# Latent-attention mixer on one core: the next head's queries and keys turned in four halves, in another PSUM bank

## The reference, cut to what matters

```python
def attend(qblk):                      # 128 queries at a time
    s = jnp.einsum('bqhd,bkhd->bhqk', qblk, k, preferred_element_type=jnp.float32) * scale
    p = jax.nn.softmax(s, axis=-1)
    return jnp.einsum('bhqk,bkhd->bqhd', p.astype(v.dtype), v)

o = lax.map(attend, qb)
...
y = jnp.einsum('bsm,md->bsd', jnp.concatenate([y_pool, y_attn], axis=-1), w_out[l])
```

## Time and profile before

| | us |
|---|---|
| median of 3 runs | 2757.69 |
| lowest, highest | 2755.79, 2765.08 |
| the profiled execution, its own time | 2761.88 |
| its span | 2760.1 |
| PE busy in the span | 2582.2 |
| DVE busy | 1772.6 |
| ACT busy | 1045.2 |
| POOL busy | 1052.5 |

### The profile page before, as it was taken

One profiled execution on the slowest core, in us unless ns is written; L12 is line 12 of the kernel. 1 busy time (PEld: TensorE's weight loads), 2 busy tenths in 40 slices (PEclk: granted clock), 3 DMA queues, 4 the chain that ended last, 5 costly groups with the idle time before them and its releaser, 6 DMA issues.

```text
span 2760.1 us, 40033 instructions
## 1 busy us (share of the span) xinstructions
PE 2582.2 (94%) x15932; PEld 2230.6 (81%) x15932; DVE 1772.6 (64%) x2506; ACT 1045.2 (38%) x1797; POOL 1052.5 (38%) x734
## 2 busy tenths in 40 slices
PE   6899999989999999999999999999999898688888
PEld 5788899966678899999998877777888786577777
DVE  6876776646433389795776346666333698777763
ACT  4322323321134332222223346666343335566651
POOL 1554554500044454554544520000344465344444
PEclk9999999999999999999999999999999999799999
DMA  6445444652024334433323374441342333000023
GB/s 237 126 173 179 139 157 141 229 205 93 24 100 154 105 109 155 142 127 107 116 91 109 115 226 123 118 131 46 122 152 100 120 114 114 1 1 1 31 77 145
DMA packets 241414, 328.09 MB, mean 119 GB/s; under 512 B 19134, under 2 KB 178110, under 8 KB 239436
## 3 DMA queue, kind: packets, MB, share of 16 engines
q1 hardware_dynamic: 239756, 325.42, 35.3%
q10 hardware_dynamic: 1472, 0.10, 0.0%
HBM read 246.16 MB, written 79.33 MB: 118 GB/s over the span
## 4 chain that ended last, share of the span: by engine, by line
PE 71%; DVE 15%; issue 6%; ACT 3%; DMA 3%; POOL 1%; SPq 0%; DVEq 0%; ACTq 0%
PE ps L851 18%; PE ps L853 18%; PE ps L852 18%; PE ps L996 4%; DVE raw L1675 3%; PE ps L984 2%; PE ps L1080 2%; DMA raw<-in_w 2%; PE ps L1060 2%; PE ps L1194 2%; PE ps L1068 1%; PE ps L1044 1%; DVE u L1689 1%; DVE st L2200 1%; PE ps L1207 1%
## 5 line engine op out<-in xcount | busy, mean ns | idle before, releaser
L807 POOL TENSOR_TENSOR w_lo<-raw,w_hi 128x512 fp32r<-128x512 f32 (+1 forms) x576 | 848.5, 1482 | 1438.1 <-ACT w_hi L1264 1437.5
L1264 ACT ACTIVATE w_hi<-raw 128x512 fp32r<-128x512 f32 (+1 forms) x580 | 357.4, 628 | 1052.1 <-PE ps L853 815.4
L851 PE MATMUL ps<-w_hi,s_hi 128*128 128x256 f32 (+1 forms) x1344 | 383.6, 285 | 10.5 <-POOL w_lo L807 10.5
L853 PE MATMUL ps<-w_hi,s_lo 128*128 128x256 f32 (+1 forms) x1344 | 381.9, 284 | 0.0
L852 PE MATMUL ps<-w_lo,s_hi 128*128 128x256 f32 (+1 forms) x1344 | 381.8, 284 | 0.0
L851 PE MATMUL ps<-w_hi,a_hi 128*128 128x256 f32 (+1 forms) x1008 | 286.2, 284 | 6.6 <-DVE a_lo L1645 4.4
L1689 DVE TENSOR_TENSOR u<-u,ps 128x1024 f32<-128x1024 f32 (+1 forms) x128 | 155.3, 1213 | 204.7 <-PE ps L853 200.8
L852 PE MATMUL ps<-w_lo,a_hi 128*128 128x256 f32 (+1 forms) x1008 | 285.9, 284 | 0.0
L853 PE MATMUL ps<-w_hi,a_lo 128*128 128x256 f32 (+1 forms) x1008 | 285.8, 284 | 0.0
L851 PEld LDWEIGHTS ps<-w_hi,s_hi 128*128 128x128 f32 x1344 | 260.1, 194 | 21.4 <-issue 19.5
L853 PEld LDWEIGHTS ps<-w_hi,s_lo 128*128 128x128 f32 x1344 | 260.1, 193 | 0.0
(11 more groups left out here) (280 smaller groups left out, 5687.1 us busy)
## 6 DMA issues: line engine op xcount, KB each, us to landing
raw<-in_w SPq DMA_DIRECT2D x191, 512.0 KB, 4.0
ada_c<-in_ada SPq DMA_DIRECT2D x14, 2304.0 KB, 10.7
blk<-u SPq DMA_DIRECT2D x62, 512.0 KB, 3.4
blk<-c SPq DMA_DIRECT2D x31, 512.0 KB, 3.3
blk<-m1s SPq DMA_DIRECT2D x31, 512.0 KB, 3.4
ada_first<-in_ada SPq DMA_DIRECT2D x12, 768.0 KB, 15.9
r_g<-blk SPq DMA_DIRECT2D x8, 1024.0 KB, 9.2
r_v<-blk SPq DMA_DIRECT2D x4, 2048.0 KB, 11.5
```

The source lines that it names most:

```text
L807: pool.tensor_tensor(w_ring(w_lo, n), w_source(n), w_ring(w_hi, n).bitcast(F32), ALU.subtract)\
L851: pe.matmul(out, a_hi_, b_hi_, start=first, stop=False, skip_group_check=True)
L853: return pe.matmul(out, a_lo_, b_hi_, start=False, stop=last, skip_group_check=True)
L1264: act.activation(w_ring(w_hi, n), w_source(n), ACT.Copy).then_inc(w_rounded, 1)
```

## The change

The queries and keys of the next head are turned in four halves of 512 tokens (queries low and high, keys low and high) at i = 2, 3, 4 and 5, each into bank 7 alone. Banks 4 and 5 hold turned probabilities alone. For the first head the four halves go to banks 4, 5, 6 and 7. Each half waits for the half before it to be read by DVE (`l_hlow`), from the third head on also for the gate of the values that bank 7 held (`l_gated`, 2h - 2). The values that go to bank 7 wait for the last half, and so do the first scores of the next head. New semaphores `l_hturned` and `l_hlow` count halves; `l_pevac` and `l_pdone` count probabilities alone.

The orders change too. PE issues scores of e + 2, then the half, then the turn of e, then the values. ACT copies the probabilities, takes the exponentials of e + 2 and then copies the half. DVE takes the maxima of e + 2, writes the probabilities' low part, inverts the sum of e + 2 and then writes the half's low part; at i = 5 (and at i = 1, where no half is turned) the gate follows.

Apart from this, the three semaphores of the DMAs of `ada_first[1]` become one, PE waits for the keys on `l_kchain` in place of `l_kdone`, and SP's wait ahead of the output weights becomes one for both halves of the last head's queries, that is at i = 3 of head 6.

```diff
-        ada_in = [[sem(f"ada_in{n}{c}") for c in range(3)] for n in range(4)]
+        ada_in = [[sem(f"ada_in{n}{c}") for c in range(3)] for n in (0, 2, 3)]
+        ada_second = sem("ada_second")
...
-        def l_head_bank(n):
-            bank = 6 if n == 1 else 4
-            return psf[0:LQK, bank * 512:bank * 512 + S].rearrange("p (m n) -> p m n", m=NT)
+        L_HALVES = {2: (0, 0), 3: (0, 1), 4: (1, 0), 5: (1, 1)}
+
+        def l_head_bank(h, k, c):
+            return ps[0:LQK, 7 if h else 4 + 2 * k + c].rearrange("p (m n) -> p m n", m=4)
+
+        def l_head_half(h, k, c, low):
+            return l_t[h % 2][k][low][0:LQK, 4 * c:4 * c + 4]
+
+        def l_half_count(h, k, c):
+            return 4 * h + 2 * k + c + 1
...
-                sp.wait_ge(l_pdone, 2 * head_unit(LH, LH - 1, 0) + 2)
+                sp.wait_ge(l_hturned, l_half_count(LH - 1, 0, 1))
...
-            for c in range(3):
-                pe.wait_ge(ada_in[1][c], 16)
+            pe.wait_ge(ada_second, 16 * 3)
...
-                pe.wait_ge(l_kdone, 1)
-
-                def l_turn_head(h, k):
-                    n = head_unit(LH, h, k)
-                    if n > 1:
-                        pe.wait_ge(l_pevac, 2 * n)
-                    for m in range(NT):
-                        tr = pe.transpose(l_head_bank(n)[:, m], (l_k if k else l_q)[:, m, h * LQK:(h + 1) * LQK],
-                                          ident[:, :])
-                    tr.then_inc(l_pdone, 2)
+                pe.wait_ge(l_kchain, 4 * NT)
+
+                def l_turn_head(h, k, c):
+                    if h:
+                        pe.wait_ge(l_hlow, l_half_count(h, k, c) - 1)
+                    if h > 1:
+                        pe.wait_ge(l_gated, 2 * h - 2)
+                    for m in range(4):
+                        tr = pe.transpose(l_head_bank(h, k, c)[:, m],
+                                          (l_k if k else l_q)[:, 4 * c + m, h * LQK:(h + 1) * LQK], ident[:, :])
+                    tr.then_inc(l_hturned, 1)
...
                     if i == 0:
-                        pe.wait_ge(l_pevac, 2 * head_unit(LH, h, 1) + 2)
+                        pe.wait_ge(l_hlow, 4 * h + 4)
...
-                    pe.wait_ge(l_pevac, 2 * prob_unit(LH, 2 * pair + 1) + 2)
+                    pe.wait_ge(l_pevac, 4 * pair + 4)
+                    if i == NT // 2 and h + 1 < LH:
+                        pe.wait_ge(l_hlow, 4 * h + 8)
...
                 for e in range(LH * NT):
                     h, i = divmod(e, NT)
-                    turned_head = h + 1 < LH and i - 1 in TURN_AT[LH]
                     if e + 2 < LH * NT:
                         l_scores(e + 2)
-                    if turned_head:
-                        l_turn_head(h + 1, TURN_AT[LH].index(i - 1))
+                    if h + 1 < LH and i in L_HALVES:
+                        l_turn_head(h + 1, *L_HALVES[i])
+                    l_turn(e)
+                    if e and e % 2 == 0:
                         l_values(e // 2 - 1)
-                        l_turn(e)
-                    else:
-                        l_turn(e)
-                        if e and e % 2 == 0:
-                            l_values(e // 2 - 1)
...
-                    if h + 1 < LH and i - 1 in TURN_AT[LH]:
-                        l_head_turned(h + 1, TURN_AT[LH].index(i - 1))
+                    l_prob_turned(e)
+                    if e + 2 < LH * NT:
                         l_exps(e + 2)
-                        l_prob_turned(e)
-                    else:
-                        l_prob_turned(e)
-                        if e + 2 < LH * NT:
-                            l_exps(e + 2)
+                    if h + 1 < LH and i in L_HALVES:
+                        l_head_turned(h + 1, *L_HALVES[i])
...
-                    if turned_head:
-                        l_head_low(h + 1, TURN_AT[LH].index(i - 1))
+                    l_prob_low(e)
+                    if e + 2 < LH * NT:
                         l_inverse(e + 2)
-                        l_prob_low(e)
-                    else:
-                        l_prob_low(e)
-                        if e + 2 < LH * NT:
-                            l_inverse(e + 2)
+                    if h + 1 < LH and i in L_HALVES:
+                        l_head_low(h + 1, *L_HALVES[i])
                     if h and i == 1:
                         l_gate(h - 1, 1)
                     if i == 5:
```

More of the change, by code:

```diff
@@ L295, in build_program @@
         (l_pads, l_sums, l_roots, l_latok, l_diff, l_ydone, l_yready, l_lturned, l_lhi, l_llo, l_rcopied,
-         l_updone, l_upfree, l_sq, l_rr, l_qdone, l_kdone, l_kchain, l_sdone, l_max, l_neg, l_exp, l_rinv, l_prob,
-         l_vhi, l_vfree, l_phi, l_half_ok, l_headhi, l_pdone, l_pevac, l_odone, l_gated) = (
+         l_updone, l_upfree, l_sq, l_rr, l_qdone, l_kchain, l_sdone, l_max, l_neg, l_exp, l_rinv, l_prob,
+         l_vhi, l_vfree, l_phi, l_half_ok, l_hturned, l_headhi, l_hlow, l_pdone, l_pevac, l_odone, l_gated) = (
             sem(n) for n in ("l_pads", "l_sums", "l_roots", "l_latok", "l_diff", "l_ydone", "l_yready",
                              "l_lturned", "l_lhi", "l_llo", "l_rcopied", "l_updone", "l_upfree", "l_sq", "l_rr",
-                             "l_qdone", "l_kdone", "l_kchain", "l_sdone", "l_max", "l_neg", "l_exp", "l_rinv",
-                             "l_prob", "l_vhi", "l_vfree", "l_phi", "l_half_ok", "l_headhi", "l_pdone", "l_pevac", "l_odone", "l_gated"))
+                             "l_qdone", "l_kchain", "l_sdone", "l_max", "l_neg", "l_exp", "l_rinv",
+                             "l_prob", "l_vhi", "l_vfree", "l_phi", "l_half_ok", "l_hturned", "l_headhi", "l_hlow", "l_pdone", "l_pevac", "l_odone", "l_gated"))
         def product_end(s, i):
@@ L632, in _ @@
                     sp.dma_start(ada_first[n][:, 3 * c:3 * c + 3], t["ada"][n][:, 3 * c:3 * c + 3])\
-                        .then_inc(ada_in[n][c], 16)
+                        .then_inc(ada_in[(0, None, 1, 2)[n]][c] if n != 1 else ada_second, 16)
             load_raw(R11, 0)
@@ L834, in _ @@
                         key_rope(m)
-                    pool.sem_inc(l_kdone, 1)
                     for e in range(LH * NT):
@@ L1191, in l_turn @@
                     for c in range(2):
-                        pe.wait_ge(l_pevac, 2 * prob_unit(LH, e) + c - 1)
+                        if e:
+                            pe.wait_ge(l_pevac, 2 * e + c - 1)
+                        else:
+                            pe.wait_ge(l_hlow, 4)
                         for n in range(4 * c, 4 * c + 4):
@@ L1210, in l_values @@
                     mm.then_inc(l_odone, 1)
-                l_turn_head(0, 0)
-                l_turn_head(0, 1)
+                for k in range(2):
+                    for c in range(2):
+                        l_turn_head(0, k, c)
                 l_scores(0)
@@ L1234, in l_between @@
                     if q == 1 and k == 0:
-                        pe.wait_ge(l_pevac, 2 * prob_unit(LH, LH * NT - 1) + 2)
+                        pe.wait_ge(l_pevac, 2 * LH * NT)
                         pe.wait_ge(l_gated, 2 * LH)
@@ L1559, in _, with l_head_turned @@
                 l_root(2 * NT - 1)
[L1561 to L1564, removed]
+                def l_head_turned(h, k, c):
+                    act.wait_ge(l_hturned, l_half_count(h, k, c))
+                    act.activation(l_head_half(h, k, c, 0), l_head_bank(h, k, c), ACT.Identity,
                                    scale=gains[0:LQK, 10 + k:11 + k]).then_inc(l_headhi, 1)
@@ L1570, in l_exps @@
                     if e >= 3:
-                        act.wait_ge(l_pdone, 2 * prob_unit(LH, e - 3) + 2)
+                        act.wait_ge(l_pdone, 2 * (e - 3) + 2)
                     act.activation(l_p[:, e % 3], psf[:, (e % 2) * 1024:(e % 2) * 1024 + S], ACT.Exp,
@@ L1578, in l_prob_turned @@
                     for c in range(2):
-                        act.wait_ge(l_pdone, 2 * prob_unit(LH, e) + c + 1)
+                        act.wait_ge(l_pdone, 2 * e + c + 1)
                         if e >= 4:
@@ L1590, in l_other_half @@
                     act.activation(l_half[l_rows(h), :], ps[l_rows(h + 1), 6 + a], ACT.Copy).then_inc(l_half_ok, 1)
-                l_head_turned(0, 0)
-                l_head_turned(0, 1)
+                for k in range(2):
+                    for c in range(2):
+                        l_head_turned(0, k, c)
                 l_exps(0)
@@ L1865, in _ @@
                     if k % 3 == 0:
-                        dve.wait_ge(ada_in[piece][k // 3], 16)
+                        dve.wait_ge(ada_in[n][k // 3], 16)
                     src = ada_first[piece][:, k]
@@ L2227, in l_gate, with l_head_low @@
                     dve.tensor_tensor(tile, high, tile, ALU.mult).then_inc(l_gated, 1)
[L2229 to L2236, removed]
+                def l_head_low(h, k, c):
+                    dve.wait_ge(l_headhi, l_half_count(h, k, c))
```

(6 more changed lines are left out.)

## The result

The changed kernel takes 2812.41 us (median of 4, 2810.34 to 2816.68) against 2756.74: 1.0201 times as long, 95% interval 1.0185 to 1.0218. The forecast had the sign, but its time was 2788.4 and its range ended at 2800: the loss is 55.7 us where 30.7 were forecast.

A forecast was written before the change was run, and what follows sets the result against it. The prediction took a chain of waits in the attention tiles to bound the kernel, no engine being full. 2761.88 + 18.2 (chain) + 12.5 (clock) = 2792.6 us profiled, less 4.2 for a median: 2788.4, range 2770 to 2800.

The forecast's parts named there:

- What bounds the kernel: Third mixer's 64 attention tiles: no engine full, a chain of waits counts; shared banks 4 and 5 make 27.9 us of them.
- The rounds: Halves at i = 2 to 5, each waiting for the one before in bank 7: 4.9 us each, 19.6 a head.
- The first scores of the next head: At i = 6 they wait for the last low part; from there to the next gate at i = 1, 18.2 us.
- The chain in sum: A head takes 37.8 us against 34.9 at full clock; seven heads, less 1.1 at each end, give +18.2 us.
- 20.4 and 12.5: Us added in attention: 20.4 for seven heads of 2.9 more, 12.5 for nine more clock falls of 1.4.
- The clock: TensorE falls to 1.2 GHz after two long pauses a head: 14 falls instead of 5, +12.5 us.
- My discount from 1.6 to 1.4: Us charged per clock fall in attention, lowered because in a round PE does only a part of the chain.
- The faster rival: Attention halves fit idle ACT and DVE time, rounds under 4.2 us overlap, 27.9 us gained: 2730 us; chance 0.05.
- The range: Whole kernel: 2770 us, without more falls and with rounds 0.2 shorter, up to 2800, nearly all falls; leaves out some 0.16.
- the case of falls after all three pauses: Attention clock also falls after the third pause, or halves are slower: 2801.5 us and up; chance 0.06.
- At no cost: Start's single DMA wait, `l_kchain` and SP's later output weight loads cost nothing; the loads at most 5.3 us if uncovered.

The follow-up runs named there:

- the two filled kernels: Throwaway transposes put into PE's pauses: the changed kernel with three pauses a head filled, 2768.6 us; the kernel before with its one pause filled, 2756.21 us.
- the best kernel: The changed kernel with the half first in ACT's and DVE's queues and bank 7 gated at i = 0: 2724.54 us, ratio 0.989.

## Why the prediction was right or wrong

*What bounds the kernel*: right. No engine was full, the chain of waits decided, and the 22.1 us of waits for the shared banks went away without a gain.

*The rounds*: right. 4.9 us against 4.79 measured at full clock. Inside, the half's copy and low part were taken too cheap, 0.60 and 0.66 against 0.68 and 0.75; the other pieces came out shorter by as much and more. The lesson of the miss is that a half of the longer copy's time, 0.55 and 0.64, is too low a guide: the time shrank less than the size.

*The first scores of the next head*: right. Pause 3.6 forecast, 3.27 measured. From rounds and head at full clock, 37.4 - 4 x 4.79 = 18.2 us remain for the rest of a head, just the 18.2 of the forecast.

*The chain in sum*: +18.2 forecast, +13.4 measured between the two filled kernels, some 11 without the fillers' own cost. The forecast counted seven heads of 2.9. Between the first and the last gate of bank 7 lie six, 2.4 longer each, +14.7; from there to the last gate the changed kernel, filled, is 2.8 shorter (24.5 against 27.3), where I took off 1.1. At the start turning to scores gave back 1.0 (2370.90 to 2376.08 is 5.2 us, before 6.2), forecast 1.1. The sum was too high, for the heads' sake. (The prediction's 20.4 and 12.5 are 20.3 and 12.6 by its own factors, which changes nothing.)

*The clock*: this step failed. Its sign and mechanism were right and its size was not. "I take a fall after each of the two long ones: 14 instead of 5, 9 x 1.4 = 12.5 us", on top of what before lost already, measured 41.8 - 6.4 = 35.4 us in the stage, some 37 without the fillers' cost. Two of its factors were too small. The count: 21 falls, three a head, the upper end that I had named, against 14. The length: by the clock of 0.81 a steady head has 2 x 0.19 x 44.4 = 17 us at 1.2 GHz, 5.6 a fall; the five falls of before come to 2 x 0.05 x 217.2 = 22 us, 4.3 a fall. The trace of before could have warned me. One of the five falls, that at 2532, lasted some 7 us (PEclk 0.57 in the window 2532:2540) and lay in the longest head, 37.3 us from gate to gate against 36.0 to 36.8 for the others. The last head, which I did not count, had two more falls.

What a us at the low clock costs did not change: 7.9 us for 22 before, and 265.2 - 224.6 = 40.6 us for 2 x 0.19 x 265.2 = 101 in the six heads from gate to gate (changed, and changed and filled), 0.4 us each time. My discount from 1.6 to 1.4, "because in a round PE does only a part of the chain", has no support in the runs.

The Trainium skill, TensorE: Matmul & The Clock Gate, section HAM oscillation, reckons the price of such falls as the throttled time times one half. In the steady head above the mean clock of 0.81 means 2 x 0.19 x 44.4 = 16.9 us at the lower level, so 8.4 us by that rule; measured 44.4 - 37.4 = 7.0, a sixth less. That PE is not the chain all the time would explain the difference; no run shows it. The rule holds here as an upper bound, and applied to the forecast pattern it would have asked for the length of each fall, which I did not estimate.

*The rivals*. The faster rival needed rounds under 4.2. With the queues reordered the chain does get there (3.4 to 4.0 us), but the gain of some 30 us appears only with the gate moved as well. Its rule, to rotate independent groups through different banks (the Trainium skill, Perfetto Trace Analysis, section Optimizing Tensor Performance), is borne out in part: the best kernel keeps probabilities and heads in different banks, though its gain is not split between banks and orders, while the halves' common bank cost nothing once the queues let it be emptied (no wait at L1181). There I had judged the common bank to be wrong, and it is not.

*The range* ended at 2800, and the case of falls after all three pauses, which came true, was put at 2801.5 and above with a chance of 0.06: its chain was too dear by some 7 us, its falls too cheap by more. That the chain's error hides a part of the clock's in the total is luck.

*At no cost*, as forecast: the start (20.90 against 20.78), SP's later loads (they land in 5.1 us, and no engine waits for them in the trace), `l_kchain` (PE waits for the queries as before).

## What to carry to other kernels

A moved operation brings its place in every queue with it: here a copy of 0.68 us that stood behind an exponential on ACT held PE through two further waits. When a change opens pauses of several us on TensorE, price them by the time that the clock stays low behind each (0.4 us for a us here), not by their number, and test the price with throwaway matmuls in the pause: if adding work makes the kernel faster, the clock was the cost. Such a filler costs its own time wherever the loop passes without a pause, here 3.3 us in the first head. Then remove the pause rather than fill it; filling gave 43.8 us, removing the waits 88.

## What the runs showed of the hardware that was not expected

Filling a pause of 3.3 or 3.4 us with useless work on the same engine gained some 3.4 us a head, 17 and 26 us in all, and the gains of two pauses added up to within 1 us.

The length of a pause alone does not tell whether the clock falls. In the changed kernel it fell at every pause of 3.3 or 3.4 us and at all seven of 1.9 us (i = 4). With the gate's pauses filled, those of 1.9 us were followed by a fall in three heads of seven; with the scores' pauses filled, one of 3.47 us was not followed by any, as one of 2.65 us in the kernel before.

From two sizes, an estimate of the part of an instruction's time that does not scale: ACT's copy of 96 partitions took 1.11 us for 1024 columns and 0.68 for 512, which on a straight line gives some 0.25 us and 0.84 ns a column; DVE's low part took 1.28 and 0.75, some 0.22 us and 1.03 ns.

DVE's last multiply of a gate, 64x512 from SBUF, takes 0.69 us where POOL does nothing, and longer where POOL's own multiply is still running. In all 13 traces it ends 0.54 or 0.55 us after POOL's whenever that one runs on for 0.13 us or more past its start: 0.68 to 0.71 us with 0.13 to 0.17 us of POOL left, 1.24 to 1.28 with 0.70 to 0.73, 1.60 to 1.62 with 1.05 to 1.08. In the head shown POOL's multiply ended at 2517.07 and the gate's at 2517.62. That it waits for POOL is read from these times; no run tried it apart. At i = 1 the multiply is 0.6 us longer for it, ahead of the half that waits for the gate.
